# Hybrid encoder step on one core: first unit's products placed among the transposes, low parts of weights in four pieces, a weight load and the rounded weights moved ahead

## The chip, the cores and the metric

The kernel runs on one core of one Trainium2 chip. Its metric is the device time of one execution in microseconds (us), the median of several runs; less is better.

## What is computed

Two layers run over 512 new frames and 32 frames of a running stream (544 rows of 1024 numbers in float32). The change touches only the head of layer 0, which is an RMS norm and one wide projection:

```python
z = rmsnorm(x, norm_mix[0]) @ w_in_ab[0]          # (544, 1024) @ (1024, 3584)
qa, ka, va, fb, ib, qb, gb = jnp.split(z, idx)    # seven parts of 512 columns
f = lbf + (1.0 - lbf) * jax.nn.sigmoid(fb)        # forget gate
logf = jnp.log(f); kb = 1.0 - f; qb = jax.nn.silu(qb)
b = jnp.cumsum(logf)                              # within blocks of 16 frames
q_dec = q * jnp.exp(b); k_in = k * jnp.exp(-b)
```

Behind it come band attention over `qa, ka, va`, the gated recurrence over `qb, kb, vb`, an output projection, a mixture of 32 experts, then layer 1 (short convolution, another mixture). All of that is the same before and after.

## The kernel before, in words

**Projection.** The 3584 columns are taken in 14 groups of 256 (`group` n, in the order of the table `GROUPS`). Each group is cut into units: 5 units of up to 128 frames where the result is wanted frame by frame (groups 0, 1 and 8 to 13), 4 units of 128 columns by 272 frames where it is wanted transposed (groups 2 to 7). A product in full precision is made of three passes over 8 slices of the contraction: rounded weights times rounded x (`wab_hi`, `xc_hi`), rounded weights times the rest of x (`wab_hi`, `xp_lo`) and the rest of the weights times rounded x (`wab_lo`, `xc_hi`): 24 matmuls in a unit, written by `unit` (lines 661 and 662). Groups 0 and 1 are the value rows `vb` of the recurrence, 2 and 3 its forget gate `fT`, 4 and 5 its query `qdecT`, 6 and 7 the output gate.

**Who prepares what.** SyncE's queue (SP) loads the weights of a group, 1 MB, into one of three buffers `wab` (`group_load`, line 336). ScalarE (ACT) rounds them into `wab_hi` (`group_hi`, line 1075). GpSimd (POOL) subtracts to get `wab_lo` (line 565), one instruction of 128x2048 for each group. For x, by chunks of 128 frames: ACT sums squares and takes the root (`square`), VectorE (DVE) scales (`norm`, line 1297, result `XN`), TensorE (PE) transposes into two PSUM banks (`norm_transpose`, line 637), ACT rounds (`mixer_in_hi`, line 1082, result `xc_hi`), DVE subtracts (`mixer_in_lo`, line 1309, result `xp_lo`).

**What sets the order.** Each engine runs its own list of instructions in program order, and counts on semaphores tie them: `z_mm` counts finished units, `w_hi` and `w_lo` count groups whose rounded and low weights are ready, `xt_a` and `xt_d` chunks whose `xc_hi` and `xp_lo` are ready, `z_free[b]` frees a PSUM bank of a unit for the unit four later. SP loads group n (from 3 on) when group n-3 has ended:

```python
            sp.wait_ge(rev_ok, 1)
            sp.dma_start(revs_dram[:, :, 0:639], ...)      # bias rows, line 353
            for n in range(3, 14):
                sp.wait_ge(z_mm, UNIT_END[n - 3])
                group_load(n)
```

`rev` is a reversed copy of the relative bias table that DVE makes (lines 1331 and 1332); line 353 writes 256 copies of its rows to DRAM, for the attention much later. `wab` of group 3 shares its buffer with group 0.

The gate's chain sits between groups 3 and 6: when group 3 has ended, DVE scales `fT` and makes `kinT` (lines 1358, 1360), ACT takes the logarithm (1101), DVE runs four scans `cumT` (1363) and four short instructions (1367 to 1372), ACT takes the exponentials (1104 to 1106), and only then ACT can take the silu of group 5, which frees the banks for group 6.

Of the kernel before, what the change touches and what calls it, by code (L numbers as in the profile page):

```python
# [14 lines left out]
F32 = mybir.dt.float32  # L15
# [4 lines left out]
ALU = mybir.AluOpType  # L20
ACT = mybir.ActivationFunctionType
AX = mybir.AxisListType

P = 128
D = 1024
KT = D // P
SEQ, DEC, PAST = 512, 32, 128
T = SEQ + DEC
NC = 5
ROWS = [128, 128, 128, 128, 32]  # L30
HALF = T // 2
NH, HD = 8, 64
# [15 lines left out]
HG = DA // 2  # L48
# [11 lines left out]
def hmoe_step(nc, x_prompt, x_sample, cache_a_k, cache_a_v, state_hgrn, state_conv, norm_mix, norm_ffn,  # L60
# [10 lines left out]
    def sem(name):  # L71
        return ctx.enter_context(nc.semaphore(name))

    with ctx:
# [59 lines left out]
        xp_lo = at("xp_lo", MISC + 20, [P, KT, T], F32R)  # L134
# [118 lines left out]
        qsq_ok = sem("qsq_ok"); qms_ok = sem("qms_ok"); qrt_ok = sem("qrt_ok"); qk_ok = sem("qk_ok")  # L253
        v_ok = sem("v_ok"); out_dma = sem("out_dma"); qkT_mm = sem("qkT_mm"); qkT_ok = sem("qkT_ok")
        rb_dma = sem("rb_dma"); bias_in = sem("bias_in");
# [64 lines left out]
        def bc(ap, shape):  # L320
            return ap.to_broadcast(shape)
# [5 lines left out]
        def _(sp):  # L327
# [4 lines left out]
            def group_load(n, parts=1):  # L332
                first = GROUPS[n // 2] * DA + (n % 2) * HG
                kt = KT // parts
                for i in range(parts):
                    sp.dma_start(wab[n % 3][:, i * kt:(i + 1) * kt, :],
                                 w_in_ab[0, i * kt * P:(i + 1) * kt * P, first:first + HG].rearrange("(k p) n -> p k n", p=P)).then_inc(wab_in[n % 3], 16)
            x_load(0)
# [12 lines left out]
            sp.dma_start(gffn[:], norm_ffn[0:1, :].partition_broadcast(P)).then_inc(gffn_in, 16)  # L351
            sp.wait_ge(rev_ok, 1)
            sp.dma_start(revs_dram[:, :, 0:639], bc(rev[:, 0:639].unsqueeze(1), [NH, 32, 639])).then_inc(rb_dma, 16)
            for n in range(3, 14):
                sp.wait_ge(z_mm, UNIT_END[n - 3])
                group_load(n)
            sp.dma_start(nk_s[0, 0, 0:PAST - DEC], cache_a_k[0, 0, DEC:]).then_inc(out_dma, 16)
            sp.dma_start(nv_s[0, 0, 0:PAST - DEC], cache_a_v[0, 0, DEC:]).then_inc(out_dma, 16)
# [156 lines left out]
        def _(pool):  # L515
# [47 lines left out]
            for n in range(14):  # L563
                pool.wait_ge(w_hi, n + 1)
                pool.tensor_tensor(wab_lo[n % 3][:], wab[n % 3][:], wab_hi[n % 3][:].bitcast(F32), ALU.subtract).then_inc(w_lo, 1)  # L565
            split.n = 14
# [45 lines left out]
        def _(pe):  # L612
# [32 lines left out]
            def unit(n, a):  # L645
# [17 lines left out]
                for k in range(KT):  # L663
                    term(wh, xc_hi, k, start=k == 0, stop=False)
                    last = term(wh, xp_lo, k, start=False, stop=False)
                    if u_ > 0:
                        last = term(wl, xc_hi, k, start=False, stop=k == KT - 1)
                if u_ == 0:
                    pe.wait_ge(w_lo, 1)
                    for k in range(KT):  # L670
                        last = term(wl, xc_hi, k, start=False, stop=k == KT - 1)
                last.then_inc(z_mm, 1)
            norm_transpose(0, 0)
            norm_transpose(0, 1)
            for c in range(NC):
                pe.wait_ge(xt_a, c + 1)
                pe.wait_ge(xt_d, c + 1)
                if c == 0:
                    pe.wait_ge(w_hi, 1)
                if c == NC - 1:  # L680
                    pe.wait_ge(tab_in, 16 * 3)
                    rows = 12 + 3 * KT
                    pe.transpose(bank[4][:, 0:rows], tab_rows[:, :], ident[0:rows, 0:rows]).then_inc(tab_mm, 1)
                unit(0, c)
                if c + 2 < NC:
                    norm_transpose(0, c + 2)
# [363 lines left out]
        def _(act):  # L1050
# [21 lines left out]
            def group_hi(n):  # L1072
                if n < 14:
                    act.wait_ge(wab_in[n % 3], 16 * (n // 3 + 1 + (n % 3 == 0)))
                    act.activation(wab_hi[n % 3][:], wab[n % 3][:], ACT.Copy).then_inc(w_hi, 1)  # L1075

            def mixer_in_hi(n, chunks=range(NC)):
# [9 lines left out]
            square(0, 0)  # L1087
            group_hi(0)
            for c in range(1, NC):
                square(0, c)  # L1090
                mixer_in_hi(0, [c - 1])
            mixer_in_hi(0, [NC - 1])
            group_hi(1)
            group_hi(2)

            act.wait_ge(lbm_ok, 1)
            act.activation(lbe[:], lbe[:], ACT.Exp).then_inc(lbe_ok, 1)
            for n in range(6):
                if n == 2:
                    act.wait_ge(f_ok, 5)  # L1100
                    act.activation(fT[:], fT[:], ACT.Ln).then_inc(ln_ok, 1)
# [5 lines left out]
                dst, fn = ((fT, ACT.Sigmoid), (qdecT, ACT.Silu), (gateT, ACT.Silu))[n // 2]  # L1107
                group_hi(n + 3)
                for b in range(4):
# [170 lines left out]
        def _(dve):  # L1280
# [33 lines left out]
            def vb_copy(hh_, c):  # L1314
                un = FIRST[hh_] + c
                dve.wait_ge(z_mm, un + 1)
                dve.tensor_copy(vb[0:ROWS[c], c, hh_ * HG:(hh_ + 1) * HG], bank[un % 4][0:ROWS[c], 0:HG]).then_inc(z_free[un % 4], 1)
            norm(0, 0)
            norm(0, 1)
            for c in range(NC):  # L1320
                mixer_in_lo(0, xp_lo, [c])
                if c + 2 < NC:
                    norm(0, c + 2)
                if c >= 2:
                    vb_copy(0, c - 2)
# [471 lines left out]
```

## Time and profile before

| | before |
|---|---|
| median of 3 runs | 1217.22 us (1215.63 to 1218.97) |
| the profiled execution: its own time | 1213.17 us |
| its span, first to last instruction | 1211.4 us |
| mean granted TensorE clock | 0.92 of full |
| TensorE matmul busy | 1019.1 us, 84% of the span |
| VectorE, ScalarE, GpSimd busy | 426.4, 289.8, 181.0 us |
| DMA | 282.83 MB, mean 233 GB/s |

The profile is one execution. Its times count from the first instruction (0) to the last (1211.4); 1.8 us of its own time lie outside the span. The projection with which this document deals lies between 0 and about 230 us.

### The profile page before, as it was taken

How to read it: one execution, taken by the hardware profiler on the slowest of the kernel's cores; microseconds unless marked ns; L12 is line 12 of the kernel's file. 1: busy time of each engine (PE TensorE's matmuls, PEld its weight loads, DVE VectorE, ACT ScalarE, POOL GpSimd, SP SyncE). 2: the span in 40 equal slices, each digit the busy share in tenths (PEclk: the TensorE clock that was granted, in tenths of full speed). 3: DMA queues.
4: the chain of work that ended last, by engine and by line, in shares of the span. 5: the costliest groups of instructions: out<-in, count | busy, mean ns of one | idle time of the engine just before them, and what ended most of it. 6: DMA issues, size and time to landing. Idle time of an engine off the chain costs nothing.

```text
span 1211.4 us, 20104 instructions
## 1 busy us (share of the span) xinstructions
PE 1019.1 (84%) x8635; PEld 797.5 (66%) x8635; DVE 426.4 (35%) x907; ACT 289.8 (24%) x551; POOL 181.0 (15%) x146
## 2 busy tenths in 40 slices
PE   4998999777999899878778289999998999778771
PEld 4988999644689765444444089999997554444440
DVE  5324475356733611111101474555436111011104
ACT  4144332114721312111101332122212211111110
POOL 4334332002000023222111000000000122221110
PEclk9999999855989999999889689999999999888896
DMA  6322221411074599999997923324566999999966
GB/s 216 83 79 70 81 98 48 96 28 53 1 262 165 232 362 417 416 416 416 416 416 302 279 45 101 105 60 150 209 106 265 364 417 416 417 416 417 414 254 231
DMA packets 114862, 282.83 MB, mean 233 GB/s; under 512 B 22954, under 2 KB 70102, under 8 KB 98356
## 3 DMA queue, kind: packets, MB, share of 16 engines
q1 hardware_dynamic: 105044, 263.66, 58.5%
q0 software_dynamic: 9728, 17.85, 4.0%
q8 instruction: 70, 1.15, 0.4%
q14 instruction: 20, 0.16, 0.0%
HBM read 270.57 MB, written 27.02 MB: 246 GB/s over the span
## 4 chain that ended last, share of the span: by engine, by line
PE 59%; DMA 24%; DVE 7%; SPq 4%; ACT 2%; issue 2%; POOL 1%; DVEq 0%; POOLq 0%; ACTq 0%
DMA w<-in_w_dram 19%; PE banks L1015 12%; PE banks L943 12%; PE banks L880 9%; PE banks L662 8%; PE banks L954 4%; PE banks L661 3%; SPq L389 3%; DMA wab<-in_w_in_ab_dram 2%; DMA yab<-y_rows 1%; PE banks L637 1%; POOL wab_lo L565 1%; PE banks L839 1%; PE banks L823 1%; PE banks L937 1%
## 5 line engine op out<-in xcount | busy, mean ns | idle before, releaser
L943 PE MATMUL banks<-w,xgT 128*64 128x256 f32 x2048 | 253.2, 406 | 74.9 <-DMA w<-in_w_dram 73.7
L943 PEld LDWEIGHTS banks<-w,xgT 128*64 128x64 f32 x2048 | 159.4, 147 | 177.3 <-DMA w<-in_w_dram 77.4
L1662 DVE TENSOR_TENSOR hh<-banks,sg 128x128 f32<-128x128 f32 x64 | 18.7, 292 | 409.1 <-ACT sg L1230 409.1
L577 POOL DMA_INDIRECT y_rows<-ys,yidx x64 | 63.7, 995 | 383.3 <-ACT ys L1238 381.9
L954 PE MATMUL banks<-w,hT 128*64 128x512 f32 x512 | 116.9, 598 | 0.0
L1015 PE MATMUL banks<-xc_hi,wc_hi 128*128 128x272 f32 x384 | 111.4, 290 | 2.1 <-DVE xc_lo L1309 2.1
L1015 PE MATMUL banks<-xc_hi,wc_lo 128*128 128x272 f32 x384 | 111.7, 291 | 0.0
L1015 PE MATMUL banks<-xc_lo,wc_hi 128*128 128x272 f32 x384 | 110.9, 289 | 0.0
L573 POOL DMA_INDIRECT xr<-x_rows,gidx x32 | 33.5, 1046 | 412.4 <-DVE yidx L1648 394.4
L662 PE MATMUL banks<-wab_hi,xc_hi 128*128 128x256 f32 (+1 forms) x320 | 91.1, 285 | 0.7 <-POOL wab_lo L565 0.7
L662 PE MATMUL banks<-wab_hi,xp_lo 128*128 128x256 f32 (+1 forms) x320 | 90.1, 282 | 0.0
L662 PE MATMUL banks<-wab_lo,xc_hi 128*128 128x256 f32 (+1 forms) x320 | 88.4, 280 | 0.0
L1230 ACT ACTIVATE sg<-banks 128x128 f32<-128x128 f32 x64 | 17.8, 278 | 295.1 <-PE banks L943 295.1
L565 POOL TENSOR_TENSOR wab_lo<-wab,wab_hi 128x2048 fp32r<-128x2048 f32 x14 | 67.3, 4816 | 121.7 <-ACT wab_hi L1075 121.7
L1015 PEld LDWEIGHTS banks<-xc_hi,wc_hi 128*128 128x128 f32 x384 | 72.9, 190 | 2.7 <-issue 2.5
L1015 PEld LDWEIGHTS banks<-xc_lo,wc_hi 128*128 128x128 f32 x384 | 72.9, 190 | 0.0
L1015 PEld LDWEIGHTS banks<-xc_hi,wc_lo 128*128 128x128 f32 x384 | 72.7, 189 | 0.0
L954 PEld LDWEIGHTS banks<-w,hT 128*64 128x64 f32 x512 | 34.0, 136 | 58.7 <-issue 54.8
L661 PE MATMUL banks<-xc_hi,wab_hi 128*128 128x272 f32 x192 | 57.0, 297 | 6.7 <-POOL wab_lo L565 6.7
L1238 ACT ACTIVATE ys<-banks 128x512 f32<-128x512 f32 x64 | 38.2, 597 | 97.9 <-PE banks L954 97.9
L661 PE MATMUL banks<-xc_hi,wab_lo 128*128 128x272 f32 x192 | 56.9, 296 | 0.0
L662 PEld LDWEIGHTS banks<-wab_hi,xc_hi 128*128 128x128 f32 (+1 forms) x320 | 55.6, 174 | 1.7 <-POOL wab_lo L565 1.0
(283 smaller groups left out, 1796.0 us busy)
## 6 DMA issues: line engine op xcount, KB each, us to landing
w<-in_w_dram SPq DMA_DIRECT2D x192, 1024.0 KB, 23.2
wab<-in_w_in_ab_dram SPq DMA_DIRECT2D x13, 1024.0 KB, 5.0
wc<-in_w_in_c_dram SPq DMA_DIRECT2D x24, 512.0 KB, 5.7
yab<-y_rows SPq DMA_DIRECT2D x16, 512.0 KB, 6.8
wo<-in_w_out_ab_dram SPq DMA_DIRECT2D x4, 1024.0 KB, 5.6
x_rows<-XF SPq DMA_DIRECT2D x8, 512.0 KB, 2.6
wo<-in_w_out_c_dram SPq DMA_DIRECT2D x4, 1024.0 KB, 5.7
H<-in_x_prompt_dram SPq DMA_DIRECT2D x4, 512.0 KB, 8.4
```

Source lines behind the costliest of these rows:

```text
L389: sp.dma_start(w13[s][:, part, :, :], w[l, bass.ds(e, 1)].rearrange("e (p k) f -> p (e k) f", p=P)).then_inc(done, 16)
L565: pool.tensor_tensor(wab_lo[n % 3][:], wab[n % 3][:], wab_hi[n % 3][:].bitcast(F32), ALU.subtract).then_inc(w_lo, 1)
L573: pool.indirect_dma_start(xr[i][:, :], None, x_dram[l][:, :], bass.IndirectOffsetOnAxis(ap=index.bitcast(U32), axis=0), bounds_check=T - 1 ...
L577: pool.indirect_dma_start(y_dram[l][:, :], bass.IndirectOffsetOnAxis(ap=index.bitcast(U32), axis=0), ys[i][:, :], None, bounds_check=4 * T ...
L661: return pe.matmul(out, w[:, k, cols], x[:, k, t], **flags)
L662: return pe.matmul(out, x[:, k, t], w[:, k, :], **flags)
L880: last = pe.matmul(bank[i % 4][0:ROWS[c], 0:OW], z(a, k)[:, c * P:c * P + ROWS[c]], w(b, k, s), start=k == 0 and j == 0, stop=k == KT - 1 ...
L943: last = pe.matmul(bank[hb][64 * f:64 * f + 64, 0:2 * P].rearrange("p (w j) -> p w j", w=2), xgT[i][:, k, 64 * ab:64 * ab + 64], w13[s][:, ...
L954: last = pe.matmul(bank[6 + ab][64 * n:64 * n + 64, :], hT[ab][:, 64 * f:64 * f + 64], w2s[s][:, f, n * 512:(n + 1) * 512], start=f == 0, ...
L1015: last = pe.matmul(bank[3 * half + a][:, 0:HALF], w[s][:, k, a, :], x[:, k, half * HALF:(half + 1) * HALF], start=k == 0 and j == 0, stop= ...
L1238: act.activation(ys[e % 4][:], bank[6 + ab][:, :], ACT.Copy).then_inc(ys_ok, 1)
L1662: dve.tensor_tensor(hh[ab][:], bank[3 + ab][:, P:2 * P], sg[ab][:], ALU.mult).then_inc(hh_ok, 1)
```

## The change

Five edits, all in the head of layer 0:

1. PE: the first unit (group 0, chunk 0) starts after the transposes of chunk 0 alone; the transposes of chunks 1 and 2 stand between its 16 products with `wab_hi` and its 8 with `wab_lo`.
2. ACT: the first group's weights are rounded in two halves, each when its half of the load has come (a new semaphore `half_in`), and chunk 0's `xc_hi` stands between them; the squares of chunks 1 and 2 follow. DVE makes `xp_lo` of chunk 0 before it scales chunk 1, and scales chunk c+1 ahead of `xp_lo` of chunk c.
3. POOL: `wab_lo` of each group is made by four instructions of 128x512 instead of one of 128x2048.
4. SP: the load of group 3 is issued when group 0 has ended, and the wait for `rev` and the write of the bias rows come after it.
5. ACT: rounding the weights of groups 1 and 3 to 6 moves ahead by one place each: group 1 between the chunks, group 3 ahead of the first sigmoids, groups 5 and 6 ahead of the waits for the logarithm and for the exponentials.

```diff
             def group_load(n, parts=1):
-                ... .then_inc(wab_in[n % 3], 16)
+                ... .then_inc(half_in if i < parts - 1 else wab_in[n % 3], 16)
...
-            sp.wait_ge(rev_ok, 1)
-            sp.dma_start(revs_dram[:, :, 0:639], bc(rev[:, 0:639].unsqueeze(1), [NH, 32, 639])).then_inc(rb_dma, 16)
             for n in range(3, 14):
                 sp.wait_ge(z_mm, UNIT_END[n - 3])
                 group_load(n)
+                if n == 3:
+                    sp.wait_ge(rev_ok, 1)
+                    sp.dma_start(revs_dram[:, :, 0:639], bc(rev[:, 0:639].unsqueeze(1), [NH, 32, 639])).then_inc(rb_dma, 16)
...
             for n in range(14):
                 pool.wait_ge(w_hi, n + 1)
-                pool.tensor_tensor(wab_lo[n % 3][:], wab[n % 3][:], wab_hi[n % 3][:].bitcast(F32), ALU.subtract).then_inc(w_lo, 1)
+                for k in range(0, KT, 2):
+                    last = pool.tensor_tensor(wab_lo[n % 3][:, k:k + 2, :], wab[n % 3][:, k:k + 2, :],
+                                              wab_hi[n % 3][:, k:k + 2, :].bitcast(F32), ALU.subtract)
+                last.then_inc(w_lo, 1)
...
                 if u_ == 0:
+                    norm_transpose(0, 1)
+                    norm_transpose(0, 2)
                     pe.wait_ge(w_lo, 1)
                     for k in range(KT):
                         last = term(wl, xc_hi, k, start=False, stop=k == KT - 1)
                 last.then_inc(z_mm, 1)
             norm_transpose(0, 0)
-            norm_transpose(0, 1)
...
                 unit(0, c)
-                if c + 2 < NC:
+                if 1 <= c and c + 2 < NC:
                     norm_transpose(0, c + 2)
...
+            def first_hi(half):
+                k = slice(half * KT // 2, (half + 1) * KT // 2)
+                act.wait_ge((half_in, wab_in[0])[half], 16)
+                return act.activation(wab_hi[0][:, k, :], wab[0][:, k, :], ACT.Copy)
...
             square(0, 0)
-            group_hi(0)
-            for c in range(1, NC):
+            first_hi(0)
+            mixer_in_hi(0, [0])
+            first_hi(1).then_inc(w_hi, 1)
+            square(0, 1)
+            for c in range(2, NC):
                 square(0, c)
                 mixer_in_hi(0, [c - 1])
+                if c == 3:
+                    group_hi(1)
             mixer_in_hi(0, [NC - 1])
-            group_hi(1)
             group_hi(2)
+            group_hi(3)
...
             for n in range(6):
+                if n > 0:
+                    group_hi(n + 3)
                 if n == 2:
                     act.wait_ge(f_ok, 5)
...
-                group_hi(n + 3)
                 for b in range(4):
...
             norm(0, 0)
+            mixer_in_lo(0, xp_lo, [0])
             norm(0, 1)
-            for c in range(NC):
+            for c in range(1, NC):
+                if c + 1 < NC:
+                    norm(0, c + 1)
                 mixer_in_lo(0, xp_lo, [c])
-                if c + 2 < NC:
-                    norm(0, c + 2)
                 if c >= 2:
                     vb_copy(0, c - 2)
```

Where the instructions stand now is shown at three places. First PE at the start of the program; the lines with `ident` are the transposes, 8 for a chunk, and the pair of `wab_hi` products stands eight times in a row in both. Of before:

```order
L637 MATMUL banks<-ident,XN 128x128 x16
L662 MATMUL banks<-wab_hi_109,xc_hi 128x256
L662 MATMUL banks<-wab_hi_109,xp_lo 128x256
...
L662 MATMUL banks<-wab_lo_106,xc_hi 128x256 x8
L637 MATMUL banks<-ident,XN 128x128 x8
```

Of the changed kernel:

```order
L641 MATMUL banks<-ident,XN 128x128 x8
L666 MATMUL banks<-wab_hi_109,xc_hi 128x256
L666 MATMUL banks<-wab_hi_109,xp_lo 128x256
...
L641 MATMUL banks<-ident,XN 128x128 x16
L666 MATMUL banks<-wab_lo_106,xc_hi 128x256 x8
```

The transposes of chunk 1 have moved from ahead of the first unit into it, and those of chunk 2 from behind it.

Second SP, from the load of the last norm weights on; `wab_103`, `_104` and `_105` are the three weight buffers. Of before, then of the changed kernel:

```order
L351 DMA gffn<-in_norm_ffn_dram 128x1024
L353 DMA rev_bias_copies<-rev 256x1x639
L336 DMA wab_103<-in_w_in_ab_dram 128x8x256
L336 DMA wab_104<-in_w_in_ab_dram 128x8x256
```

```order
L351 DMA gffn<-in_norm_ffn_dram 128x1024
L336 DMA wab_103<-in_w_in_ab_dram 128x8x256
L357 DMA rev_bias_copies<-rev 256x1x639
L336 DMA wab_104<-in_w_in_ab_dram 128x8x256
```

The load of group 3 has passed the bias rows; that of group 4 still stands behind them.

Third ACT around the logarithm and the exponentials, from the sigmoids of group 3 on (`wab_hi_111` there is group 5's, `wab_hi_109` group 6's). Of before:

```order
L1113 ACTIVATE fT<-banks 128x272 x4
L1101 ACT_TABLE_LOAD
L1101 ACTIVATE fT<-fT 128x2176
L1075 ACTIVATE wab_hi_111<-wab_105 128x2048
L1113 ACT_TABLE_LOAD
L1113 ACTIVATE qdecT<-banks 128x272 x4
L1104 ACT_TABLE_LOAD
L1104 ACTIVATE fT<-cumT 128x2176
L1105 ACTIVATE cumT<-cumT 128x2176
L1106 ACTIVATE dec<-dec 128x136
L1075 ACTIVATE wab_hi_109<-wab_103 128x2048
```

Of the changed kernel:

```order
L1129 ACTIVATE fT<-banks 128x272 x4
L1080 ACTIVATE wab_hi_111<-wab_105 128x2048
L1118 ACT_TABLE_LOAD
L1118 ACTIVATE fT<-fT 128x2176
L1129 ACT_TABLE_LOAD
L1129 ACTIVATE qdecT<-banks 128x272 x4
L1080 ACTIVATE wab_hi_109<-wab_103 128x2048
L1121 ACT_TABLE_LOAD
L1121 ACTIVATE fT<-cumT 128x2176
L1122 ACTIVATE cumT<-cumT 128x2176
L1123 ACTIVATE dec<-dec 128x136
```

Both roundings have moved from behind the function that waits for DVE to ahead of it.

## Rows read from the trace of the kernel before

**Rows 1.** The page: span, granted TensorE clock in 40 slices
```profile
span 1211.4 us, 20104 instructions
...
PEclk9999999855989999999889689999999999888896
```

**Rows 2.** Waits, 0 to 235: total, times, longest (us)
```profile
PE banks L661 <- POOL wab_lo L565: 6.7, 3, 3.0
```

**Rows 3.** Timeline of PE: start, us, what, [idle before <-releaser]
```profile
17.24 1.97 PE L637 MATMUL banks<-ident,XN 128*128 128x128 f32 x8 [7.30 <-DVE XN L1297]
...
37.45 0.39 PE L662 MATMUL banks<-wab_hi,xc_hi 128*128 128x256 f32 x1 [0.74 <-POOL wab_lo L565]
...
66.81 0.40 PE L661 MATMUL banks<-xc_hi,wab_hi 128*128 128x272 f32 x1 [2.86 <-POOL wab_lo L565]
...
108.94 0.59 PE L661 MATMUL banks<-xc_hi,wab_hi 128*128 128x272 f32 x1 [3.01 <-POOL wab_lo L565]
```

**Rows 4.** Windows of PE: stretch, length, busy (instructions), granted clock, DMA share, GB/s
```profile
51.90:63.95 12.05, 12.04 (x96) 1.00 0.55 151
66.80:80.70 13.90, 13.89 (x98) 0.88 0.12 40
...
69.00:71.00 2.00, 2.00 (x10) 0.50 0.00 0
```

**Rows 5.** Chain that ended last, 0 to 320: start, us, what
```profile
22.54 0.88 PE banks L637 x8
23.42 2.85 PE banks L662 x24
...
108.94 25.92 PE banks L661 x192
134.86 59.48 PE banks L662 x504
...
238.67 4.60 issue
```

**Rows 6.** Timeline of DVE
```profile
13.12 4.07 DVE L1297 SCALAR_TENSOR_TENSOR XN<-H,rstd,gmix 128x1024 f32<-128x1024 f32 x1
17.11 1.28 DVE L1309 TENSOR_TENSOR xp_lo<-banks,xc_hi 128x512 fp32r<-128x512 f32 x2
...
18.49 1.28 DVE L1297 SCALAR_TENSOR_TENSOR XN<-H,rstd,gmix 128x1024 f32<-128x1024 f32 x1
...
89.08 5.61 DVE L1363 TENSOR_TENSOR_SCAN cumT<-reset,fT 128x544 f32<-128x544 f32 x1
...
106.49 4.69 DVE L1378 TENSOR_TENSOR qdecT<-qdecT,fT 128x2176 f32<-128x2176 f32 x1 [2.01 <-ACT qdecT L1113]
```

**Rows 7.** Timeline of POOL
```profile
4.03 0.29 POOL L519 TENSOR_SCALAR_AFFINE_SELECT upper<-upper 128x128 f32<-128x128 f32 x1
...
11.60 4.50 POOL L565 TENSOR_TENSOR wab_lo<-wab,wab_hi 128x2048 fp32r<-128x2048 f32 x1 [0.89 <-ACT wab_hi L1075]
...
88.54 5.00 POOL L565 TENSOR_TENSOR wab_lo<-wab,wab_hi 128x2048 fp32r<-128x2048 f32 x1 [17.27 <-ACT wab_hi L1075]
103.90 11.73 POOL L565 TENSOR_TENSOR wab_lo<-wab,wab_hi 128x2048 fp32r<-128x2048 f32 x2 [10.37 <-ACT wab_hi L1075]
```

**Rows 8.** Timeline of ACT
```profile
9.61 1.91 ACT L1075 ACTIVATE wab_hi<-wab 128x2048 fp32r<-128x2048 f32 x1 [3.79 <-DMA wab<-in_w_in_ab_dram]
11.43 1.04 ACT L1060 ACTIVATE junk<-H 128x1024 bf16<-128x1024 f32 x1
...
97.89 2.02 ACT L1104 ACTIVATE fT<-cumT 128x2176 f32<-128x2176 f32 x1 [3.41 <-DVE cumT L1372]
```

**Rows 9.** DMA issues in 43.1 to 43.3, then in 104 to 107 (us to landing last)
```profile
wab<-in_w_in_ab_dram SPq DMA_DIRECT2D x1, 1024.0 KB, 17.0
...
wab<-in_w_in_ab_dram SPq DMA_DIRECT2D x1, 1024.0 KB, 5.0
```

**Rows 10.** DMA issue in 1.6 to 2.0: the first half of group 0
```profile
wab<-in_w_in_ab_dram SPq DMA_DIRECT2D x1, 512.0 KB, 6.4
```

More of the change, by code:

```diff
@@ L253, in hmoe_step @@
         qsq_ok = sem("qsq_ok"); qms_ok = sem("qms_ok"); qrt_ok = sem("qrt_ok"); qk_ok = sem("qk_ok")
-        v_ok = sem("v_ok"); out_dma = sem("out_dma"); qkT_mm = sem("qkT_mm"); qkT_ok = sem("qkT_ok")
+        v_ok = sem("v_ok"); out_dma = sem("out_dma"); half_in = sem("half_in"); qkT_mm = sem("qkT_mm"); qkT_ok = sem("qkT_ok")
         rb_dma = sem("rb_dma"); bias_in = sem("bias_in");
@@ L336, in group_load @@
                     sp.dma_start(wab[n % 3][:, i * kt:(i + 1) * kt, :],
-                                 w_in_ab[0, i * kt * P:(i + 1) * kt * P, first:first + HG].rearrange("(k p) n -> p k n", p=P)).then_inc(wab_in[n % 3], 16)
+                                 w_in_ab[0, i * kt * P:(i + 1) * kt * P, first:first + HG].rearrange("(k p) n -> p k n", p=P)).then_inc(half_in if i < parts - 1 else wab_in[n % 3], 16)
             x_load(0)
@@ L1073, in group_hi @@
                 if n < 14:
-                    act.wait_ge(wab_in[n % 3], 16 * (n // 3 + 1 + (n % 3 == 0)))
+                    act.wait_ge(wab_in[n % 3], 16 * (n // 3 + 1))
                     act.activation(wab_hi[n % 3][:], wab[n % 3][:], ACT.Copy).then_inc(w_hi, 1)
+            def first_hi(half):
+                k = slice(half * KT // 2, (half + 1) * KT // 2)
+                act.wait_ge((half_in, wab_in[0])[half], 16)
+                return act.activation(wab_hi[0][:, k, :], wab[0][:, k, :], ACT.Copy)
             def mixer_in_hi(n, chunks=range(NC)):
```

## The prediction

> **What bounds it now.** I read the page first: 84% of the span PE is busy, and the granted clock dips in the third to fifth slice of 30 us, before the attention [rows 1]. Then the waits of the first 235 us: of PE's waits for weights, three belong to line 661, 6.7 us in total [rows 2]. The timeline of PE gives their places: group 1 waits 0.74 us, group 3 2.86 us at 66.81, group 6 3.01 us at 108.94, so 6.7 - 2.86 - 3.01 = 0.8 us are left for group 5; before the first unit PE idles 7.30 us for the scaled chunk 1 [rows 3]. The windows show what a pause of some 3 us costs beyond itself: behind it the granted clock is 0.50 of full (1.2 GHz), 10 matmuls take 2.00 us (0.20 each), where 96 take 12.05 us (0.126 each) at 1.00 (2.4 GHz) [rows 4]. So group 3 (66.80 to 80.70, two rows of the next group in it) takes 1.8 us more than group 2, and the two groups from 108.94 on take 25.92 us in the chain of waits [rows 5] where 2 x 12.05 = 24.1 are due: 1.8 us again. From 134.86 on PE runs 59.48 us in one piece [rows 5].
>
> Each wait ends with `wab_lo`, but three different things are late. Group 3: its load, issued at 43.2 behind the bias rows, took 17.0 us to land, where a load alone takes 5.0 [rows 9]; rounding and `wab_lo` follow only from 60.2 on. Group 6: ACT rounds behind the exponentials, which start at 97.89 after waiting for DVE [rows 8], so POOL starts at 103.90 [rows 7]. Chunk 1: the scaling at 13.12 takes 4.07 us, though the same instruction takes 1.28 at 18.49 [rows 6]; POOL's `wab_lo` runs from 11.60 to 16.10 [rows 7], and 16.1 + 1.1 is where it ends.
>
> Everything behind 229 us starts on events of the projection, so a microsecond saved here is one at the end, unless a later wait depends on something else.
>
> **The start.** Who goes first where DVE and POOL both want to work is in the rows. The POOL instruction of 88.54 takes 5.00 us instead of 4.50, and the scan of 89.08 takes 5.61 us, of which POOL's 4.5 leave 1.1 for its work; at 106.49 DVE's product takes 4.69, and the second of two POOL instructions from 103.90 is the longer by 2.2 us [rows 6, 7]: 103.90 + 4.99 = 108.89, DVE runs to 111.2, POOL follows. So each waits for the whole instruction of the other, and at its end the one that waits gets in. The Trainium skill ("SBUF — State Buffer", on who interferes with whom) calls this an exclusive lock for DVE instructions with two SBUF inputs, held for a whole instruction; it doesn't say who follows when both want it. By that rule the pieces cut both ways: DVE gets in sooner and `wab_lo` comes later, 18.7 instead of 16.2 in the sum below; since PE's transposes end at 18.4 anyway, that costs 0.3 us of the sum.
>
> A piece of 128x512: at least 4.50 / 4 = 1.13 us; at most that plus the 0.29 us that a whole POOL instruction of 128x128 takes, 1.42 [rows 7]. I take 1.15: that short instruction has 128 columns of work in its 0.29, so that little is left for its start. The Trainium skill ("GPSIMD Engine Reference", performance versus the Vector engine) gives 2.6 cycles an element and a dispatch in two software hops for each instruction, 1.11 us and the dispatch, as an estimate from its figures; the sum doesn't use it.
>
> In order: the first half of group 0's weights lands at 1.7 + 6.4 = 8.1 [rows 10]; ACT's half takes 1.05 (a square of 128x1024 takes 1.04 and rounding 128x2048 1.91 [rows 8]), then `xc_hi` of chunk 0 to 10.5 and the second half to 11.5. DVE's `xp_lo` of chunk 0 (1.28 [rows 6]) ends at 11.85. PE starts the 16 products at 11.9, at half clock, 0.2 each: 15.2. The root of chunk 1 comes at 12.9; DVE's scaling waits for the piece that ends at 13.9 and ends at 15.1. Transposes 15.2 to 16.2 (0.9 at full clock [rows 5], 1.97 at half [rows 3]). Chunk 2's scaling waits for the third piece, 16.25 to 17.5, transposes to 18.4; fourth piece to 18.7; 8 products to 19.7. The next unit starts there; before it started at 23.4 less 0.2 for its first product, 23.2 [rows 5]. **Gain 3.5 us.** Bounds: at 1.42 a piece it is 1.1 less; if PE stays at half clock through the pauses, the transposes take 1.1 longer, the 8 products 0.7 and the second unit 2.0 (24 x 0.2 against 2.85): nothing, about, is left.
>
> Behind it chunk 3 is scaled at 20.4, chunk 4 at 25.4 (it waits for one piece of group 1), `xp_lo` of chunk 3 at 26.7, and PE asks for it at 26.9: no wait, but 0.2 us from one. Group 1's pieces are done at 27.7 and PE ends group 0 at 33.0, so the 0.74 us go too. **Gain 0.7.** PE enters group 1 at 33.1 instead of 37.45.
>
> **Group 3.** With group 1 ended at 47.5 and group 2 at 59.5, group 3 needs its weights at 59.5. The load is issued at 33.1, lands 5.0 to 17.0 later [rows 9], at worst at 50.1; rounding 1.9 and pieces 4.6 make 56.6. Even the worst is hidden. **Gain 2.86 + 1.8 = 4.7.** What is queued behind SP's wait for `rev`: group 4's load. `rev` is made at about 35, the load is due at 47.5. With 17.0 us it lands at 64.5, is rounded at 66.4, subtracted at 71.1, and needed at 71.6: covered, with 0.5 us to spare in the worst case and 10 in the likely one. ACT, held by the early rounding of group 3, has nothing else to do between 29.4 and 38.
>
> **Groups 5 and 6.** Count from the end of group 3, at 71.6. ACT rounds group 5 first (0.4 to 2.35), POOL's pieces follow; one of them can stand ahead of `kinT`, so the logarithm starts 1.1 us later than before, at 5.0. But the scans no longer wait 4.3 us for one whole POOL instruction, one piece at most: the last short DVE instruction ends at 15.3 instead of 97.9 - 80.7 = 17.2 [rows 8, 4]. Group 6 is rounded at 12.45 to 14.35, inside ACT's wait; exponentials and table 15.6 to 20.3, first silu done at 22. The bank is needed at 24.1, and `wab_lo` of group 6 comes at about 20. `wab_lo` of group 5 comes at 9.7 and is needed at 12.05. **Gain 0.8 + 3.0 + 1.8 = 5.6.** Cover: 2.1 us at the exponentials, 2.3 at group 5.
>
> From group 7 on, the order is as before. The pieces make POOL's part some tenths longer, covered by about 6 us (group 7's ended at 103.90 + 11.73 = 115.6 [rows 7] and was needed when group 6 ended, about 121.7); DVE's short instructions wait for a piece instead of a whole instruction.
>
> **Sum:** 3.5 + 0.7 + 4.7 + 5.6 = 14.5 us. The profiled execution has 1213.17 us, so it would have 1198.7 (span 1196.9); the median of the runs lies 4.05 above that execution. I take the sum off the median: 1217.2 - 14.5 = 1202.7 us. A change under 0.3% (3.7 us) can't be told from none.
>
> **Rivals.**
> - *DVE and POOL collide in the gate's chain.* Four short DVE instructions follow the scans, each tied to the one before. If group 6's pieces start at the same moment, each may wait 1.15 us: 15.3 becomes 19.9, the first silu 26.6 instead of 22, and PE pauses 2.5 us and runs at half clock behind it, 1.8 more. For it: the starts lie 1 us apart. Against: POOL starts at 14.4, when three of the four are over. 1204 to 1207; 12 in 100.
> - *The start gives nothing.* The chain of pauses at 16.2 to 17.5 keeps the half clock. 1205 to 1206; 14 in 100.
> - *POOL runs its four pieces ahead of a waiting DVE.* The two hand-overs near 89.0 and 108.9 speak against it. Chunk 1 is scaled at 17.5, the second unit starts at 20.8, 1.1 us less: 1203.8; 6 in 100.
> - *More comes back than counted,* where a later stage gets another clock or the 4.60 us in which PE waits for nothing that the profile shows, at 238.67 [rows 5], fall away: 1198; 6 in 100.
> - *The gain is given back later,* in a transfer that doesn't start on an event of the projection. I find none; 1214 to 1218; 4 in 100.
> - *The other side: the clock.* PE would now run from 20 to 215 us without a pause. If the chip answers with half clock, each group of 12.05 us costs as much again; from (14.5 + 3.7) / 12.05 = 1.5 groups on the kernel is slower, at two groups 1227. Against: the 59.48 us in one piece [rows 5], in slices that read 9 [rows 1]. 3 in 100.
>
> My forecast has 55 in 100, its own range 1200.5 to 1205. The range 1199 to 1208.5 takes in the first three rivals and leaves out the others. Faster 0.93 (all but the last two), same 0.04, slower 0.03.
>
> **What would show it.** In the changed profile: the second unit near 19.7 and group 1 near 33.1; the scaling of chunk 1 under 2.5 us; no wait of PE for `wab_lo` beyond 1 us and granted clock 1.00 from 20 to 215; SP's loads of groups 4 to 6 near 47.5, 59.5, 71.6; the exponentials ending near 20 us behind group 3; the piece of line 662 that ended at 134.86 + 59.48 = 194.3 ending near 180. I am wrong if PE waits in front of group 6 or 4, if group 1 starts less than 4 us earlier, or if from the end of that piece to the end of the span it takes longer than the 1017.1 us (1211.4 - 194.3) of before.

## The result

The changed kernel takes 1197.96 us (median of 4 runs, 1195.77 to 1200.30), the kernel before took 1216.77 us beside it (4 runs, 1215.63 to 1218.97): ratio 0.9844, 95% interval 0.9819 to 0.9868. It is faster, as forecast, but the time lies 1.0 us below the range of 1199 to 1208.5, and 4.7 us below the forecast of 1202.7. The profiled execution took 1198.60 us, with a span of 1196.9 us; 1198.7 and 1196.9 were forecast for it. One execution in the experiments, a run of experiment 10, took 2517.45 us, more than twice as long as its five neighbours (1193.0 to 1199.2), and stands in no comparison.

The page of the changed kernel, its span and its granted clock [rows 1]:

```profile
span 1196.9 us, 20147 instructions
...
PEclk9999999657899999988889599999999999888895
```

The chain that ended last, in the first 320 us (start, us, what) [rows 5]:

```profile
11.59 6.97 POOL wab_lo L567 x4
18.60 4.07 PE banks L666 x32
22.67 0.87 PE banks L641 x8
23.55 2.85 PE banks L666 x24
...
27.00 3.03 PE banks L666 x24
30.21 17.03 PE banks L666 x144
47.24 72.47 PE banks L665 x576
119.71 59.48 PE banks L666 x504
```

Between 30.21 and the end of the projection PE waits for nothing. The 576 products of groups 2 to 7 take 72.47 us, 0.126 each, at full clock throughout. The piece of 504 products, which started at 134.86, starts at 119.71: 15.15 us earlier, where the sum said 14.5. Of PE's waits in the first 220 us none is for POOL any more [rows 2]:

```profile
PE banks L641 <- DVE XN L1313: 8.9, 2, 8.0
...
PE banks L666 <- DVE xp_lo L1325: 2.1, 1, 2.1
```

The timelines of DVE, POOL, ACT and SP show the steps of the prediction one by one. DVE [rows 6]:

```profile
13.10 2.09 DVE L1313 SCALAR_TENSOR_TENSOR XN<-H,rstd,gmix 128x1024 f32<-128x1024 f32 x1
...
15.30 2.11 DVE L1313 SCALAR_TENSOR_TENSOR XN<-H,rstd,gmix 128x1024 f32<-128x1024 f32 x1
...
74.03 2.27 DVE L1377 TENSOR_SCALAR kinT<-fT 128x2176 f32<-128x2176 f32 x1
...
85.17 1.28 DVE L1389 TENSOR_TENSOR cumT<-cumT,dec 128x1088 f32<-128x1088 f32 x1
```

POOL, where x4 is one group's low part in four pieces [rows 7]:

```profile
11.59 6.96 POOL L567 TENSOR_TENSOR wab_lo<-wab,wab_hi 128x512 fp32r<-128x512 f32 x4 [0.87 <-ACT wab_hi L1085]
...
29.19 5.03 POOL L567 TENSOR_TENSOR wab_lo<-wab,wab_hi 128x512 fp32r<-128x512 f32 x4 [1.80 <-ACT wab_hi L1080]
```

ACT [rows 8]:

```profile
87.02 2.03 ACT L1121 ACTIVATE fT<-cumT 128x2176 f32<-128x2176 f32 x1
```

SP's queue at groups 3 and 4:

```profile
33.14 0.38 SPq L336 DMA_DIRECT2D wab<-in_w_in_ab_dram  x1
34.66 0.86 SPq L357 DMA_DIRECT2D rev_bias_copies<-rev  x1
47.27 0.39 SPq L336 DMA_DIRECT2D wab<-in_w_in_ab_dram  x1
```

The scaling of chunk 1 takes 2.09 us instead of 4.07, one piece of POOL's between. Group 0's pieces take 6.96 us, since two scalings stand among them; a low part that nobody disturbs takes 5.03 in four, against 4.5 to 4.6 in one. The exponentials start at 87.02 instead of 97.89. The load of group 3 goes out at 33.14 and lands in 5.0 us.

So the head went as written. What remained open was the time: the two profiled executions differ by 14.6 us, the medians by 18.8 (16.1 to 22.0 by the interval of the ratio).

### The profile page after: what moved, and what is told of

Its sections match the earlier page's. It is cut to its first block, busy times and chain, and to the rows that moved or that the text cites. A ratio compares the mean times of both kernels' runs of the same rounds, so it can differ in the third digit from the quotient of the medians.

```text
span 1196.9 us, 20147 instructions
## 1 busy us (share of the span) xinstructions
PE 1014.1 (85%) x8635; PEld 793.2 (66%) x8635; DVE 409.5 (34%) x907; ACT 291.4 (24%) x552; POOL 191.1 (16%) x188
## 3 DMA queue, kind: packets, MB, share of 16 engines
q8 instruction: 70, 1.15, 0.4%
## 4 chain that ended last, share of the span: by engine, by line
PE 62%; DMA 25%; DVE 6%; SPq 2%; issue 2%; ACT 1%; POOL 1%; another core or an unknown queue 0%; DVEq 0%; POOLq 0%; ACTq 0%
DMA w<-in_w_dram 22%; PE banks L1020 12%; PE banks L948 12%; PE banks L666 9%; PE banks L885 9%; PE banks L665 6%; PE banks L959 3%; SPq L390 2%; DMA yab<-y_rows 1%; PE banks L641 1%; PE banks L844 1%; PE banks L828 1%; PE banks L811 1%; PE banks L756 1%; PE banks L942 1%
## 5 line engine op out<-in xcount | busy, mean ns | idle before, releaser
L1679 DVE TENSOR_TENSOR hh<-banks,sg 128x128 f32<-128x128 f32 x64 | 18.7, 292 | 408.7 <-ACT sg L1246 408.7
L567 POOL TENSOR_TENSOR wab_lo<-wab,wab_hi 128x512 fp32r<-128x512 f32 x56 | 77.5, 1414 | 96.4 <-ACT wab_hi L1080 95.5
L666 PEld LDWEIGHTS banks<-wab_hi,xp_lo 128*128 128x128 f32 (+1 forms) x320 | 56.2, 176 | 0.4
```

The costliest lines, as they stand in the source:

```text
L567: last = pool.tensor_tensor(wab_lo[n % 3][:, k:k + 2, :], wab[n % 3][:, k:k + 2, :], wab_hi[n % 3][:, k:k + 2, :].bitcast(F32), ALU.subtract)
L666: return pe.matmul(out, x[:, k, t], w[:, k, :], **flags)
L1679: dve.tensor_tensor(hh[ab][:], bank[3 + ab][:, P:2 * P], sg[ab][:], ALU.mult).then_inc(hh_ok, 1)
```

## The experiments

Each kernel is timed beside the kernel before. "The piece" is the run of 504 products of line 662 of before; its start tells what the projection lost or gained. Experiments 1 to 4 ran together, so did 5 to 8 and 9 to 12.

### 1 and 2. Both kernels once more

No edit. Expected of the kernel before:

> The kernel before, unchanged, profiled once more. Both theories are about the 4.3 us by which the measured gain (18.8 us of the medians) is larger than the gain of the two profiled executions (1213.17 - 1198.60 = 14.6 us). Theory 1, an execution out of the spread: the profiled execution of before was a lucky one, and nothing in its stages is shorter for a reason; a second profile then gives 1214 to 1219 us, with the projection (end of the 59.48 us piece of line 662) at 194 as before and the rest of the difference scattered behind it. Theory 2, a wait that varies: the wait of group 3 for its load beside the bias rows (17.0 us to landing) is usually longer, by some 4 us; a second profile then shows group 3 starting near 71 instead of 66.81 and the piece ending near 198.

Expected of the changed kernel:

> The changed kernel, unchanged, profiled once more. Both theories: 1196 to 1200 us, the piece of line 666 ending at 179.2 within 0.3, since nothing in the projection waits for a transfer any more. Theory 1: the ratio to before comes out nearer to 14.6 / 1217 = 0.988. Theory 2: it stays at 0.9845.

Measured: the kernel before has a median of 1210.9 us over 20 runs (1206.3 to 1215.3) as reference and 1212.6 over 12 runs (1210.1 to 1215.8) as experiment, ratio 1.0009 (0.9995 to 1.0022). Its profile gives 1213.40 us, with the piece at 135.03:

```profile
67.00 13.87 PE banks L661 x96
109.11 25.93 PE banks L661 x192
135.03 59.48 PE banks L662 x504
```

The changed kernel: 1196.7 us, ratio 0.9874 (0.9851 to 0.9897), the piece at 119.70.

This rules out the second theory. Group 3 starts at 67.0, not at 71, so no wait of the head varies by 4 us: over these runs and the first ones the head of either kernel repeats within 0.2 us. Of the first theory the stages hold and the number doesn't: it had 1214 to 1219 us for a second profile of before, and 1213.40 came, like the first one's 1213.17. So it was not the profiled execution that stood apart but the set beside it. The gain is 1 - 0.9874 = 1.26% of 1210.9, 15.3 us (12.5 to 18.0 by the interval), which agrees with what the head gives. The 1217 us of the first set are what stands out: three later sets of the kernel before have medians of 1210.9, 1211.2 and 1211.4.

### 3. The order on SP alone

```diff
-            sp.wait_ge(rev_ok, 1)
-            sp.dma_start(revs_dram[...], ...)
             for n in range(3, 14):
                 sp.wait_ge(z_mm, UNIT_END[n - 3])
                 group_load(n)
+                if n == 3:
+                    sp.wait_ge(rev_ok, 1)
+                    sp.dma_start(revs_dram[...], ...)
```

> Before, with the load of group 3 issued ahead of the bias rows and nothing else changed. Theory 1: the pause of 2.86 us in front of group 3 and the 1.8 us at half clock behind it go, 4.7 us less in the trace, 1212 us as a median (ratio 0.996). Theory 2: the pause is usually longer than in the one trace, so the timed gain is 8 to 9 us (ratio 0.993). The pauses in front of groups 5 and 6 stay in both.

Measured: ratio 0.9960 (0.9944 to 0.9976), 4.8 us by the ratio and 4.4 between the medians; the piece at 129.20, 5.66 us earlier. That is the first theory's number in the time; in the trace it is 1 us more than it said: group 1 starts 0.5 us later, and the 1.5 us of half clock behind the last pause don't come this time, though the pause ahead of group 6 is 3.01 us long as before:

```profile
103.00:104.70 1.70, 0.00 (x0) 1.00 0.96 304
104.70:106.00 1.30, 1.23 (x9) 1.00 1.07 374
106.00:108.00 2.00, 2.00 (x18) 1.00 0.05 15
```

(Columns as in [rows 4].) 18 products begin in 2 us, where before 10 did behind the same pause.

### 4. The changed kernel without the order on SP

```diff
             for n in range(3, 14):
                 ...
-                if n == 3:
-                    sp.wait_ge(rev_ok, 1)
-                    sp.dma_start(revs_dram[...], ...)
```
and both lines ahead of the loop, as before.

> The changed kernel, with the bias rows issued ahead of the load of group 3 as before. The table rev is made by 34.6 already, so the load goes out at 35.6; with 17.0 us to landing it is there at 52.6, rounded at 54.5, subtracted at 59.5, and group 3 wants it at 59.4. Theory 1: a pause of 0 to 0.5 us, time that of the changed kernel within 1 us. Theory 2, landing some 4 us later than 17.0 as a rule: a pause of 3 to 5 us and half clock behind it, 1201 to 1204 us.

Measured: ratio 0.9874 (0.9854 to 0.9893), as the changed kernel; the piece at 120.14, 0.4 us later. The load of group 3 lands in 16.8 us and no pause follows. The first theory holds again, and one term of the sum gets another owner: with the other edits in place SP's order is worth 0.4 us, not 4.7.

### 5. The changed kernel with the low parts whole

```diff
-                for k in range(0, KT, 2):
-                    last = pool.tensor_tensor(wab_lo[n % 3][:, k:k + 2, :], ...)
-                last.then_inc(w_lo, 1)
+                pool.tensor_tensor(wab_lo[n % 3][:], ...).then_inc(w_lo, 1)
```

> The changed kernel with each low part as one POOL instruction again. Theory 1, the pieces carry the gate's chain: with group 5 rounded ahead of the logarithm, POOL's 4.5 us stand ahead of kinT, which then ends at 79.5 instead of 76.3; the last short instruction follows 3 to 6 us later than in the changed kernel (86.4), because the low part of group 6 now stands in one piece among the scans and the short instructions; PE pauses 3 to 5 us ahead of group 6. With 1.1 us at the start, 4 to 8 us slower than the changed kernel, so 1201 to 1205 where that takes 1197. Rival, the pieces matter only while chunks 1 and 2 are scaled: 1.1 us slower, no pause ahead of group 6.

Measured: ratio 0.9944 (0.9921 to 0.9966), 8.5 us slower than the changed kernel by the ratios; the piece at 126.45, 6.7 us later. DVE in the gate's chain:

```profile
77.34 5.59 DVE L1374 TENSOR_SCALAR kinT<-fT 128x2176 f32<-128x2176 f32 x1
85.02 4.84 DVE L1377 TENSOR_TENSOR_SCAN cumT<-reset,fT 128x544 f32<-128x544 f32 x4 [2.09 <-ACT fT L1115]
89.89 4.43 DVE L1381 COPY dec<-cumT 128x68 f32<-128x68 f32 x1
```

A copy of 68 numbers a partition takes 4.43 us, because POOL's instruction of 89.44 got in just ahead of it; `kinT` takes 5.59 instead of 2.27 in the changed kernel (1.29 in before). PE pauses 2.9 us ahead of group 6, as the view of its waits puts it, for ACT's silu:

```profile
PE banks L662 <- ACT qdecT L1126: 2.9, 1, 2.9
```

Another 3.3 us are lost at the start (the 144 products begin at 33.52 instead of 30.21), where 1.1 was expected. Most of it is lost before the second unit, which starts at 22.01 instead of 19.65: chunk 1 is scaled by 17.2 instead of 15.2, PE pauses 1.76 us for it, and from 18.5 to 21.8 its granted clock is 0.50. The transposes of chunk 2 and the 8 low products take almost twice their 1.09 and 1.21 us:

```profile
18.63 1.97 PE L638 MATMUL banks<-ident,XN 128*128 128x128 f32 x8 [0.30 <-DVE XN L1310]
20.25 1.92 PE L663 MATMUL banks<-wab_lo,xc_hi 128*128 128x256 f32 x8
```

The rest is chunk 4's scaling, which takes 4.16 us behind the low part of group 1, which now stands between the chunks; PE waits 0.8 us for it. The rival falls.

### 6. The pieces alone

```diff
-                pool.tensor_tensor(wab_lo[n % 3][:], ...).then_inc(w_lo, 1)
+                for k in range(0, KT, 2):
+                    last = pool.tensor_tensor(wab_lo[n % 3][:, k:k + 2, :], ...)
+                last.then_inc(w_lo, 1)
```

> Before, with the low parts in four pieces and nothing else changed. Theory 1, a good part of what the sum put down to the load's order comes from the pieces, since DVE's copy of the table rev (4.76 us behind POOL before) is done at once: the load of group 3 goes out near 38.5 instead of 43.2, lands near 55.5, and the pause ahead of group 3 shrinks from 2.9 to 0.5 us; chunk 1 is scaled 1.8 us sooner; ahead of group 5 the pause grows by 1 to 2 us, as scans and pieces alternate. 4 to 6 us faster than before. Rival: POOL's part only gets longer and the pauses grow, 0 to 3 us slower than before.

Measured: ratio 0.9948 (0.9925 to 0.9971), 6.3 us faster than before; the piece at 128.37, 6.5 us earlier. SP issues the bias rows at 38.01 and the load at 38.91 instead of 42.25 and 43.16, and no pause is left ahead of group 3. Ahead of group 5 the pause grows from 0.8 to 3.2 us, where scans and pieces alternate:

```profile
81.12 6.93 DVE L1366 TENSOR_TENSOR_SCAN cumT<-reset,fT 128x544 f32<-128x544 f32 x4 [2.09 <-ACT fT L1104]
88.08 1.10 DVE L1370 COPY dec<-cumT 128x68 f32<-128x68 f32 x1
89.21 1.19 DVE L1371 COPY dec<-cumT 128x68 f32<-128x68 f32 x1
```

The half clock follows it (288 products in 37.98 us instead of 36.2), and the pause ahead of group 6 is gone, as PE comes there later. A little more than expected, by the mechanism expected. In the traces the edit that looks like a mere cutting-up is the largest single one; by the time it isn't clear of the load's order alone (3.5 to 9.1 us against 2.9 to 6.8).

### 7. The start alone

Edits 1 and 2 on the kernel before; in short:

```diff
+                    norm_transpose(0, 1)       # inside unit(0, 0), ahead of the low products
+                    norm_transpose(0, 2)
...
-            group_hi(0)
+            first_hi(0)
+            mixer_in_hi(0, [0])
+            first_hi(1).then_inc(w_hi, 1)
```

> Before, with the first unit among the transposes, the half loads and DVE's order (edits 1 and 2) and nothing else. POOL's instruction for group 0 stands whole from 11.6 to 16.1, chunk 1 is scaled at 17.4, chunk 2 at 18.9, the second unit starts at 20.8 instead of 23.2: 2.4 us faster than before, the pauses ahead of groups 1, 3, 5 and 6 all stay. Rival, POOL's whole instruction takes back what the order gives: under 1 us.

Measured: the piece at 131.81, 3.05 us earlier, in which the missing half clock behind the last pause is 1.5 (24.42 us for two groups instead of 25.92) and 1.6 us come from the start (group 1 at 35.87 instead of 37.45). The time can't tell it from no change: ratio 0.9988 (0.9969 to 1.0007). I had 2.4 for the start. Chunks 1 and 2 are scaled at 17.2 and 18.6, no later than expected (17.4 and 18.9), yet the second unit starts at 21.68 instead of 20.8, since the 16 transposes ahead of it run at the pace of half clock and take 3.65 us, where the changed kernel's two lots of 8 take 1.04 and 1.09:

```profile
17.23 3.65 PE L637 MATMUL banks<-ident,XN 128*128 128x128 f32 x16 [1.55 <-DVE XN L1306]
```

### 8. The early roundings alone

Edit 5 on the kernel before:

```diff
                 mixer_in_hi(0, [c - 1])
+                if c == 3:
+                    group_hi(1)
...
-            group_hi(1)
             group_hi(2)
+            group_hi(3)
...
+                if n > 0:
+                    group_hi(n + 3)
                 if n == 2:
```

> Before, with the roundings of groups 1, 3, 5 and 6 ahead (edit 5) and nothing else. The load of group 3 still lands at 60.2, so the pause there stays, larger by the 0.7 us that the pause ahead of group 1 gives back. Group 5's whole low part now stands ahead of kinT and makes the logarithm 4 us later. Ahead of group 6 the pause is about 2 us instead of 3.0. 1 to 2.5 us faster than before. Rival, the late logarithm costs more than the early rounding gives: the exponentials come at 101.5 or later and the kernel is as before or slower.

Measured: the piece at 131.13, 3.7 us earlier; ratio 0.9977 (0.9949 to 1.0004), not to be told from no change. The expectation was wrong in its parts. Group 1's whole low part runs from 25.98 to 30.56 and holds up chunk 4's scaling, in the chain of waits:

```profile
27.49 4.16 DVE XN L1300
```

PE pauses 1.7 and 0.9 us for this chunk and then runs at a granted clock of 0.50 from 34.0 to 37.4 (1.6 us). So group 0 ends 4.4 us later, and the pause ahead of group 3 is used up there rather than gone: group 3 starts 0.3 us later than before (67.13), but at full clock, and group 4 starts 1.3 us earlier (79.21 instead of 80.50). Ahead of group 5 there is no pause (0.8 back), ahead of group 6 one of 2.9 us with no half clock behind it (24.39 us for two groups, 1.5 back).

### 9. The changed kernel with the roundings behind the exponentials

```diff
             for n in range(6):
-                if n > 0:
-                    group_hi(n + 3)
                 if n == 2:
...
+                if n > 0:
+                    group_hi(n + 3)
                 for b in range(4):
```

> The changed kernel with the roundings of groups 5 and 6 behind the logarithm and behind the exponentials as before; groups 1 and 3 stay ahead. Theory 1: the rounding of group 5 starts at 77.3 instead of 71.7, its pieces alternate with the scans and end near 85.5, where PE wants them at 83.3: a pause of 2 us. The rounding of group 6 ends near 95, its pieces near 100.5, wanted at 97.5: 3 us. 5 us later at the end of the projection, 119.7 becomes 124.7, plus 0 to 1.8 us for each pause that the half clock follows: 1202 to 1205 where the changed kernel takes 1197. Rival, with POOL in pieces the order at the exponentials doesn't matter any more: within 1 us.

Measured: the piece at 124.70, 5.0 us later. That is the number expected, from other parts: a pause of 3.2 us ahead of group 5 and half clock behind it (288 products in 38.02 us instead of 36.2); ahead of group 6 none, since PE comes later there. Waits, then windows:

```profile
PE banks L665 <- POOL wab_lo L567: 3.2, 1, 3.2
```

```profile
83.00:86.60 3.60, 0.48 (x4) 1.00 0.55 180
86.70:88.70 2.00, 2.00 (x10) 0.60 0.52 183
```

The time: 1198.6 us, where 1202 to 1205 was expected; ratio 0.9905 (0.9871 to 0.9939), 3.7 us slower than the changed kernel by the ratios; the interval takes in 0 as well as 8. The profiled execution has a span of 1196.7 us, as the changed kernel's, though its head is 5.0 us longer. This is the clearest case of what spreads. The start of the second output projection, the last stage but the mixture, in before, the changed kernel and this one (median and extremes in ns, first and last start in us):

```profile
L880 PE MATMUL banks<-wo_hi,g_hi x160: 276/278/363, 851.4 to 910.8; 128*128 128x256 f32 x128, 128*32 128x256 f32 x32
```

```profile
L885 PE MATMUL banks<-wo_hi,g_hi x160: 275/279/365, 836.3 to 897.0; 128*128 128x256 f32 x128, 128*32 128x256 f32 x32
```

```profile
L885 PE MATMUL banks<-wo_hi,g_hi x160: 276/278/365, 841.3 to 899.8; 128*128 128x256 f32 x128, 128*32 128x256 f32 x32
```

From there to the end of the span it takes 1211.4 - 851.4 = 360.0 us before, 360.6 in the changed kernel and 355.4 here, with the same code. Over all 14 traces this stretch, which is the second mixture with that projection, has 355.4 to 361.3 us; the first mixture with the projection ahead of it 364.0 to 367.2; the stretch of layer 1 between them 147.7 to 149.4. Most of the spread sits in the mixtures, where the experts' weights stream in; why it varies there no run shows.

### 10. A version with an earlier low part

```diff
-            first_hi(0)
+            first_hi(0).then_inc(half_hi, 1)
...
+            pool.wait_ge(half_hi, 1)
+            low(0, (0, 2))                 # two pieces, ahead of POOL's last constants
+            pool.wait_ge(w_hi, 1)
+            low(0, (4, 6)).then_inc(w_lo, 1)
```

> The changed kernel, with POOL's first two pieces of group 0 waiting only for the first half of the rounded weights (9.3 instead of 11.6) and standing ahead of the last constants that POOL writes. Theory 1, at the start PE now waits for the low part and for DVE behind it: the fourth piece ends at 16 instead of 18.56, chunk 2 is scaled near 17, the second unit starts 0.5 to 1 us sooner than at 19.6. Rival, DVE's scalings are the later ones and move back by a piece: no gain, up to 0.5 us later. The time can't tell these apart, the trace can.

Measured: the pieces run undisturbed from 9.46 to 14.44; the 8 low products start at 17.81 instead of 18.60, as the first theory has it:

```profile
16.96 1.10 PE L647 MATMUL banks<-ident,XN 128*128 128x128 f32 x8 [0.30 <-DVE XN L1319]
17.81 1.19 PE L672 MATMUL banks<-wab_lo,xc_hi 128*128 128x256 f32 x8
```

Of the 0.8 us half is lost again at `xp_lo` of chunk 3 (0.27 us) and around it: the piece starts at 119.28 instead of 119.71. Ratio 0.9871 (0.9842 to 0.9900), not to be told from the changed kernel's 0.9874. It doesn't beat it by anything that can be measured.

### 11 and 12. Two pieces, eight pieces

```diff
-                for k in range(0, KT, 2):
+                for k in range(0, KT, 4):      # two pieces; eight: range(0, KT, 1)
```

Expected of two pieces:

> The changed kernel with two pieces of 128x1024 for each low part instead of four. Theory 1, what DVE waits for is the length of one POOL instruction, 2.35 us here: chunk 2 is scaled at 18.8 instead of 17.4 and the second unit starts 1 us later; in the gate's chain kinT ends 1.1 us later and the scans wait once for 2.35 us, the exponentials start near 89 instead of 87.0, which the 2 us of cover just about hold: end of the projection 120.7 to 122. Rival, the number of hand-overs counts and not the length: the same as with four, within 0.3 us.

Expected of eight:

> The changed kernel with eight pieces of 128x256. One piece of 128x512 took 1.26 us alone and four took 5.03 where one whole took 4.56, so each further instruction costs 0.16: eight take 5.7. Theory 1: DVE waits 0.7 us at most, but the low part of group 0 comes later, as two scalings still stand between: 18.56 becomes 19 to 19.3, the second unit starts 0.5 us later, and nothing else pauses: projection ends at 120.2, within 0.7 us of four pieces. Rival: more hand-overs let DVE in earlier and the start gains: 0.3 to 0.8 us sooner.

Measured: the piece starts at 120.38 with two and 120.64 with eight, against 119.71 with four; ratios 0.9877 (0.9844 to 0.9909) and 0.9876 (0.9843 to 0.9908), the same as with four. With two, chunk 2's scaling takes 3.19 us; with eight 1.56, but group 0's low part ends at 19.13 and PE waits 0.8 us for it:

```profile
11.63 7.50 POOL L567 TENSOR_TENSOR wab_lo<-wab,wab_hi 128x256 fp32r<-128x256 f32 x8 [0.92 <-ACT wab_hi L1085]
```

In both the first theory's direction holds and its number is off by a little: 120.7 to 122 was expected of two, and within 0.7 us of four pieces of eight, which is 0.9 later. The rivals (the same within 0.3 us; 0.3 to 0.8 us sooner) fall. The step from one piece to two is what matters (6.1 of 6.7 us), and four is a flat optimum in the traces.

## Why the prediction was right and wrong

**The head: right, term by term.** The second unit starts at 19.6 (19.7 said), group 1 at 32.95 (33.1), group 3's load at 33.14 (33.1) and landed in 5.0 us, SP's next load at 47.27 (47.5), chunk 1 scaled at 15.19 (15.1), the low part of group 0 at 18.55 (18.7), the last short instruction at 86.45, 15 us behind group 3 (15.3), the piece ends at 179.2 ("near 180"). The sum of 14.5 us is 15.15 in the trace and 15.3 by the ratio of experiment 2. The three rivals inside the head are gone: the exponentials leave cover; the transposes of chunk 1 take 1.04 us, so the start is at full clock from 15.5 on; and chunk 1 is scaled at 15.19 and not at 17.5, so POOL doesn't run its pieces ahead of DVE. The rival of the clock is gone too, as PE is granted full clock from 20 to 214 us. One hit is a cancellation: the pieces take 0.43 us more than 4 x 1.15, and the two scalings among them add 1.93 us (6.96 - 5.03) where the sum had 2.45.

Two readings ahead of the sum don't stand. The slices of [rows 1] read 9 up to the seventh and show no dip before the attention; it is the windows [rows 4] that show it. And "at half clock" for PE's first products is a reading of their pace, 0.21 us each: the granted clock of that stretch (12.0 to 15.4 in the changed kernel) is recorded as 1.00.

**The hand-over between POOL and DVE: right.** Each waits for the other's instruction to end, and the one that waits gets in there; experiments 5, 11 and 12 show that the length of the piece bounds the wait: chunk 2's scaling takes 3.19, 2.11 and 1.56 us with two, four and eight. What is waited for is the rest of the piece that runs, so chunk 1's scaling takes 1.94 us with two pieces and 2.09 with four. A piece takes 1.26 us, not 1.15 (the upper end was 1.42). The Trainium skill ("SBUF — State Buffer", on who interferes with whom) names copies and products with a scalar among the DVE instructions that can take the shared ports, where their operands allow it, and the traces agree: 4.43 us for a copy of 68 numbers, 5.59 for `kinT`, a product with a scalar (both in experiment 5).

**The step that failed: "I take the sum off the median".** The profiled execution of before lay 4.05 us below the median of its three runs. I treated this as a fixed distance and forecast 1202.7 from the median, not 1198.7 from the execution on which every term rests. Experiment 1 shows that the distance is no property of the kernel: one more profile gives 1213.40 us, among runs with medians of 1210.9 and 1212.6, so it lies 0.8 to 2.5 us above its medians and not 4.05 below. The changed kernel's median, 1197.96 us, lies 0.64 below its profiled execution. Single runs of the same kernel go from 1206.3 to 1219.8 us. My range took in only errors of the sum and hardly any of this; with 1198.7 as the centre, 1198.0 is a hit to 0.7 us. That it is so close is partly luck: the repeat of experiment 2 has a median of 1196.7. Why the first set of before stood 6 us above the three later ones is open: it has only one trace, and that one isn't longer.

**The number of a rival, not its mechanism.** "More comes back than counted" had 1198 us, which is what was measured. What it named didn't happen: the wait in which PE waits for nothing that the profile shows is still there, in the chain of the changed kernel,

```profile
223.49 4.82 issue
```

the granted clock is 0.50 for some 65 us behind the projection in both traces, and from the end of the piece to the end of the span it takes 1017.7 us instead of 1017.1. By the letter that last number is one of the signs of being wrong; at 0.6 us it is far inside what this stretch varies by (in experiment 2 it takes 1016.3).

**A cause that was given to one edit alone.** I put 4.7 us to the load's order on SP. Experiments 3 and 4 show that it gives this alone (4.8 us by the ratio) and 0.4 us beside the others, and experiment 6 that the pieces alone remove the same pause, since what delayed SP was DVE's copy of `rev`, 4.76 us behind POOL. The gains of the four edits alone, 5.7, 6.5, 3.1 and 3.7 us in the traces, make 18.9 where all together give 15.15. The sum stayed right because each pause was counted once.

**A price that isn't fixed.** 1.8 us of half clock behind each pause of 3 us was in the sum twice. It is there in both profiles of before, in experiments 6 and 9 (ahead of group 5) and in experiment 7 ahead of group 3, and it is missing in experiments 3, 5, 7 and 8, behind pauses of 2.9 to 3.0 us ahead of group 6. So it follows seven of the eleven pauses of 2.9 to 3.2 us in these traces. The sum came out because both traces of the kernel before have it at both places. Half clock also follows shorter pauses, of 1.76 us at the start of experiment 5 and of 1.7 and 0.9 in experiment 8. What decides it these runs don't show. The price was a little high too: behind the pause ahead of group 6 two groups take 25.92 us at first half and then full clock, and 24.39 to 24.43 us where full clock follows (experiments 3, 7 and 8). That makes 1.5 us; the sum had compared them with groups that follow no pause.

## What to carry to other kernels

Here a GpSimd instruction was a wait of up to its whole length, 4.5 us, for VectorE's scalings, copies and scans alike, and for all that is tied behind them; cutting it in two to four pieces costs 0.16 us for each further piece and was, in the traces, the largest of the edits. A pause that ends several waits has several cures: undo each edit in the full version as well as doing it alone, before a gain is put down to one. A difference read from one trace belongs on that trace's own time, and the range around it must hold the spread of the medians, here some 6 us between sets.

## What was not expected of the hardware

A pause of PE of some 3.0 us is followed by 1.2 GHz in some kernels (0.60 mean granted clock over 86.70 to 88.70 in experiment 9) and by 2.4 GHz in others (1.00 over 104.70 to 108.00 in experiment 3), some 1.5 us apart; experiment 7 has both in one trace (0.50 over 65.10 to 68.50, 1.00 over 107.30 to 111.00). The two mixtures spread by 3.2 and 5.9 us from trace to trace with the same code; the projection of either kernel, in its two traces, by 0.2.
